# Even mixer of a hybrid encoder: gate weights folded with the block-diagonal ones, v turned by its product, tiles and heads in another order, values centred before attention

## The reference, cut to what matters

```
u_m, z_m, u_r, g_r = _split(x @ w_in, EVEN_SIZES)          # 4 x 1024
# mLSTM half
c = silu(dw_conv(u_m, conv_w, conv_b))
q, k, v = blockdiag(c, wq), blockdiag(c, wk) / 16, blockdiag(u_m, wv)   # blocks of 4
qkv = concatenate([q, k, v], axis=-1)
i_pre = einsum('bld,rdh->rbhl', qkv, w_ig) + b_ig           # r: two directions, h: 4 heads
log_f = log_sigmoid(einsum('bld,rdh->rbhl', qkv, w_fg) + b_fg)
h = chunkwise attention with decays from log_f, i_pre, forward plus backward
y_m = sigmoid(z_m) * head_norm(h, norm_g, ML_HEADS, center=True)        # minus mean, over root of variance
# RG-LRU half
x = dw_conv(u_r, ...); r, i = sigmoid(blockdiag64(x, w_a) + b_a), sigmoid(blockdiag64(x, w_x) + b_x)
a = exp(-8 r softplus(-lam)); h = a h_before + sqrt(1 - a*a) * i * x    # both directions
y_r = (h_f + h_b) * gelu(g_r)
return concatenate([y_m, y_r], axis=-1) @ w_out
```

## Time and profile before

| | |
|---|---|
| time, median of 3 runs | 2589.86 us (2588.8 to 2591.7) |
| the profiled execution | 2589.05 us, its span 2587.3 us |
| mean granted clock of TensorE | 0.982 of 2.4 GHz |
| busy in the span | PE 98%, PEld 81%, DVE 50%, ACT 35%, POOL 40% |
| chain that ended last | PE 85%, DVE 8%, ACT 4%, issue 2% |

### The profile page before, as it was taken

One profiled execution on the slowest core, in us unless ns is written; L12 is line 12 of the kernel. 1 busy time (PEld: TensorE's weight loads), 2 busy tenths in 40 slices (PEclk: granted clock), 3 DMA queues, 4 the chain that ended last, 5 costly groups with the idle time before them and its releaser, 6 DMA issues.

```text
span 2587.3 us, 32687 instructions
## 1 busy us (share of the span) xinstructions
PE 2530.2 (98%) x11838; PEld 2089.5 (81%) x11838; DVE 1283.3 (50%) x1519; ACT 902.0 (35%) x1178; POOL 1047.4 (40%) x484
## 2 busy tenths in 40 slices
PE   8999999999999999999999999999999999999998
PEld 7888887776767888888888888888888788788887
DVE  3333357666566433235333245676777566433335
ACT  3223236675232322213222214444544332422222
POOL 6444453221123544445444445333333333544443
PEclk9999999998999999999999999999999999999999
DMA  4222222111112222322222322222222222222222
GB/s 153 97 97 98 101 70 72 64 62 43 47 49 73 82 94 94 108 95 73 98 97 97 102 98 93 74 74 75 73 74 74 69 78 85 78 97 97 98 101 78
DMA packets 63676, 218.75 MB, mean 85 GB/s; under 512 B 10925, under 2 KB 15021, under 8 KB 63457
## 3 DMA queue, kind: packets, MB, share of 16 engines
q1 hardware_dynamic: 63120, 216.03, 24.5%
q0 software_dynamic: 464, 1.45, 0.2%
HBM read 215.36 MB, written 2.10 MB: 84 GB/s over the span
## 4 chain that ended last, share of the span: by engine, by line
PE 85%; DVE 8%; ACT 4%; issue 2%; POOL 1%; DMA 0%; DVEq 0%; POOLq 0%; ACTq 0%; SPq 0%
PE ps L485 24%; PE ps L486 24%; PE ps L487 24%; PE ps L516 2%; PE ps L935 2%; DVE sb_cv L1737 1%; DVE sb_th L1761 1%; DVE sb_lx L1737 1%; DVE sb_rec L1863 1%; ACT sb_th L1295 1%; PE ps L642 1%; PE ps L641 1%; PE ps L640 1%; PE ps L646 1%; DVE sb_x L1659 1%
## 5 line engine op out<-in xcount | busy, mean ns | idle before, releaser
L394 POOL TENSOR_TENSOR sb_wl<-sb_raw,sb_wh 128x1024 fp32r<-128x1024 f32 (+1 forms) x376 | 974.2, 2591 | 1468.9 <-ACT sb_wh L1108 1468.9
L1108 ACT ACTIVATE sb_wh<-sb_raw 128x1024 fp32r<-128x1024 f32 (+1 forms) x376 | 419.4, 1115 | 1326.7 <-PE ps L487 1264.1
L485 PE MATMUL ps<-sb_xh,sb_wh 128*128 128x512 f32 x2096 | 835.2, 398 | 0.9 <-DVE sb_rq L1986 0.5
L487 PE MATMUL ps<-sb_xl,sb_wh 128*128 128x512 f32 x2096 | 820.4, 391 | 0.0
L486 PE MATMUL ps<-sb_xh,sb_wl 128*128 128x512 f32 x2096 | 820.4, 391 | 0.0
L485 PEld LDWEIGHTS ps<-sb_xh,sb_wh 128*128 128x128 f32 x2096 | 396.6, 189 | 89.5 <-issue 4.6
L487 PEld LDWEIGHTS ps<-sb_xl,sb_wh 128*128 128x128 f32 x2096 | 396.0, 189 | 83.9
L486 PEld LDWEIGHTS ps<-sb_xh,sb_wl 128*128 128x128 f32 x2096 | 396.5, 189 | 82.4 <-issue 3.1
L1571 DVE SCALAR_TENSOR_TENSOR sb_hf<-sb_sg,ps 128x512 f32<-128x512 f32 x88 | 60.5, 688 | 589.8 <-PE ps L487 567.1
L485 PE MATMUL ps<-sb_hh,sb_wh 128*128 128x512 f32 x616 | 239.7, 389 | 0.5 <-POOL sb_wl L394 0.5
L487 PE MATMUL ps<-sb_hl,sb_wh 128*128 128x512 f32 x616 | 239.7, 389 | 0.0
(11 more groups left out here) (337 smaller groups left out, 2980.6 us busy)
## 6 DMA issues: line engine op xcount, KB each, us to landing
sb_raw<-w_in SPq DMA_DIRECT2D x176, 512.0 KB, 3.2
sb_raw<-w_out SPq DMA_DIRECT2D x64, 704.0 KB, 4.0
sb_raw<-w_od SPq DMA_DIRECT2D x80, 512.0 KB, 3.2
sb_raw<-w_ev SPq DMA_DIRECT2D x40, 512.0 KB, 3.2
sb_raw<-w_evo SPq DMA_DIRECT2D x8, 512.0 KB, 3.2
sb_raw<-w_odo SPq DMA_DIRECT2D x8, 512.0 KB, 3.2
sb_x<-x_in SPq DMA_DIRECT2D x8, 256.0 KB, 5.7
out<-sb_x SPq DMA_DIRECT2D x16, 128.0 KB, 1.8
```

The lines of the kernel that those rows point to most:

```text
L394: pool.tensor_tensor(wl[:, sl.par, 0:n], raw[:, sl.par, 0:n], wh[:, sl.par, 0:n].bitcast(F32), ALU.subtract).then_inc(lo_done, 1)
L485: pe.matmul(out, w_h, rh(k), start=start and k == 0, stop=False)
L487: mm = pe.matmul(out, w_h, rl(k), start=False, stop=stop and k == kt - 1)
L1108: act.activation(wh[:, sl.par, 0:kt * P], raw[:, sl.par, 0:kt * P], ACT.Copy).then_inc(hi_done, 1)
```

## The change

The gate products are q·w, k·w and v·w with q = c·wq and so on, so the weights are multiplied once: `wf` holds wq·w + wk·w/16 for c, and wv·w for u_m. It is made by VectorE once, behind the first feed-forward input phase, from a table `wgs` that replaces `wg`. For each tile VectorE copies 32 weights per channel into `gw`, spread so that each gate kind starts at its own partition of 32, and TensorE does two products of 512 columns with them. The gate sums arrive as rows in bank 6, and need no transpose. v is made with `um` as stationary operand and `bd` as moving one, so that it comes out by token, without `vf` and transposes. The tile order is new: slot m of tile t, LRU gate products, slot u of tile t + 1, slot g, inner products; the slots and transfers are dealt in that order. On ScalarE the four tanh stand ahead of Silu, and the stores of q, k, v at the tile's end; on VectorE the scans of a tile follow in the same tile. The mean of a head over its channels is taken out of `vT` (`value_centre`: weights in attention are the same for all channels of a head), so `head_mean` and `head_cen` go. ScalarE stores the head as `k_all`, and its square as `q_all`, straight from PSUM, and VectorE adds the two halves of the square (`square_sum`), so that `head_var` has one product. The slots of z and of the output product lie elsewhere among the heads, keys × queries of the next head stand behind the attention product, and z has two buffers.

```diff
+                def inner(t):
+                    bq, bk, bv = QKV_BANKS
+                    u = um[:, :, 2:2 + L]
+                    pe.wait_ge(bd_done, t + 1)
+                    pe.wait_ge(c_done, t + 1)
+                    pe.wait_ge(u_ev, t + 1)
+                    pe.wait_ge(lt_done, 4 * t + 2)
...
+                    pe.matmul(ps[:, 6, :], gw[:, 0, :], cc[:], start=t == 0, stop=False)
+                    pe.matmul(ps[:, 6, :], gw[:, 1, :], u, start=False, stop=t == KD - 1)
                     for b in range(NB):
+                        o = 2 + (b % SB) * P
+                        mm = pe.matmul(ps[:, bv, b * P:(b + 1) * P], um[:, b // SB, o:o + P], bd[:, 2, :],
+                                       start=True, stop=True)
+                    mm.then_inc(vt_mm, 1)
...
+                    else:
+                        pe.wait_ge(u_ev, t)
+                        of_x(0, sl(ev_m(t)))
+                        lru_gates(t)
+                        if t < KD - 1:
+                            pe.wait_ge(lu_ev, t + 1)
+                            of_x(1, sl(ev_u(t + 1)))
+                        pe.wait_ge(gelu_done, t)
+                        of_x(2, sl(ev_g(t)))
+                    inner(t)
...
+                def value_centre(h):
+                    v = vT[:, :, HT * h * P:HT * (h + 1) * P]
+                    dve.wait_ge(vt_ev, HT * h + HT)
+                    step(dve.tensor_reduce(vmean[:], v, mybir.AxisListType.X, ALU.add))
+                    step(dve.tensor_scalar(vmean[:], vmean[:], 1.0 / (HT * P), None, ALU.mult))
+                    step(dve.tensor_tensor(v, v, vmean[:, :, None].to_broadcast([P, NB, HT * P]), ALU.subtract))
...
+            def head_var(c, bank, src):
+                pe.wait_ge(rsq_done, c + 1)
                 pe.wait_ge(hv_done, c + 1)
+                pe.matmul(ps[:, bank, :], cn("mean_256"), src, start=True, stop=True).then_inc(hvar_mm, 1)
...
+            def square_sum(c, sq):
+                dve.wait_ge(hsq_done, c + 1)
+                dve.tensor_tensor(sq[:, 0, :], sq[:, 0, :], sq[:, 1, :], ALU.add).then_inc(rsq_done, 1)
...
                 for h in range(NH):
                     if h >= 1:
                         pe.wait_ge(hv_done, h)
...
-                    if h >= 1:
-                        head_mean(h - 1, 6, hv, lambda: None)
...
+                    if h == 0:
+                        early_out(1)
+                    elif h == 1:
+                        pe.wait_ge(part_in, 3)
+                        early_out(4)
...
+                    else:
+                        early_out(6)
                     pe.wait_ge(att_done, h + 1)
...
+                    if h < NH - 1:
+                        if h >= 1:
+                            pe.wait_ge(hvar_in, h)
+                        keys_queries(h + 1)
                 pe.wait_ge(z_done, 7)
+                early_out(7, (0, 3))
+                pe.wait_ge(hvar_in, NH - 1)
+                head_var(NH - 1, 7, q_all[:, HT * (NH - 1), :])
+                early_out(7, (3, KD))
```

More of the change, by code:

```diff
@@ L144, in build @@
     lgl = sb("lgl", [P, T], F32, e1)
[L145 removed]
+    e1[0] += 256
     e2 = [e1[0]]
@@ L357, in _, with slot @@
                 elif kind == "even":
+                    def slot(j):
+                        load(slot_of(a["w_ev"], j), KD, Slot(n0, 0, 2, j))
                     for t in range(KD):
-                        for j in (EV_U(t), EV_M(t), EV_G(t)):
-                            load(slot_of(a["w_ev"], j), KD, Slot(n0, 0, 2, j))
+                        if t == 0:
+                            slot(ev_u(0))
+                        slot(ev_m(t))
                         if t == 0:
@@ L368, in _ @@
                                                "c g d -> c g d")).then_inc(bd_in, 16)
+                        for j in sorted([ev_g(t)] + ([ev_u(t + 1)] if t < KD - 1 else [])):
+                            slot(j)
                     stream(a["w_ev"], 3 * KD, 2 * KD, KD, n0 + 3 * KD)
@@ L1270, in even @@
                     act.activation(lum[:, :, 2:2 + L], seqs(ps[:, 1, :]), ACT.Copy).then_inc(lu_ev, 1)
-                    if t >= 1:
-                        decay_root(t - 1)
-                        gelu(t - 1)
-                    split(KD, sl(EV_G(t)))
-                    if t >= 1:
-                        v_turned(t - 1)
-                    used(sl(EV_M(t)))
+                lru_in(0)
+                for t in range(KD):
+                    last = t == KD - 1
+                    if t == 0:
+                        split(KD, sl(2))
+                    used(sl(ev_m(t)))
                     if t == 0:
@@ new lines, in even @@
+                    if t == 0:
+                        split(KD, sl(4))
+                    decay(t)
+                    if not last:
+                        lru_in(t + 1)
+                        split(KD, sl(ev_u(t + 1) + 2))
+                    decay_root(t)
+                    if not last:
+                        gelu(t)
+                        if t >= 1:
+                            split(KD, sl(ev_g(t) + 2))
+                        inner_out(t)
+                    else:
+                        split(KD, sl(ev_g(t) + 2))
@@ L1328, in even @@
                 act.activation(g2[:], g1[:], ACT.Ln, bias=1.0).then_inc(rows_a, 1)
+                for d in range(2):
+                    y = 64 * d
+                    act.activation(gi[:, d, :], ps[y:y + NH, 6, :], ACT.Identity, bias=gb[y:y + NH, 0:1]).then_inc(rows_a, 1)
+                inner_out(KD - 1)
                 split(KD, sl(EV_F[0]))
                 gelu(KD - 1)
+                split(KD, sl(EV_F[1]))
                 act.wait_ge(gT_mm, 1)
@@ L2022, in ret @@
                     dve.wait_ge(rz_done, r + 1)
-                    head_norm(c, 7, rhv, rrec[:], "ret_g", HT * r, rzs, yhB, ylB)
+                    head_norm(c, 7, rhv[:], rrec[:], "ret_g", HT * r, rzs, yhB, ylB)
                     if more:
```

372 lines of the change are left out of this document (170 added, 202 removed).

## The result

The changed kernel takes **2570.16 us** (median of 4 runs, 2568.5 to 2572.8) against 2589.86: a ratio of 0.9926, with a 95% interval of 0.9913 to 0.9938. That is 19.7 us less, where 28.8 were forecast. It lies inside the range (2544 to 2572), near its upper end.

The account below looks back on a forecast made before the run. The prediction took TensorE to bound the kernel nearly everywhere, with slack in the VectorE and ScalarE loop. Tiles −10.0, hand-over −0.8, heads −18.0 and start 0 gave −28.8, about 2561 us against 2589.86; range 2544 to 2572.

Parts of the forecast that it names:

- Tiles, −10.0: Even mixer's eight tiles: seven rounds save 6.4 us and the first tile 3.6, together 10.0 us less.
- the first tile gains more: First tile: three evictions no longer ahead of Exp, 1.4, and only two stalls, 2.2, so 3.6 us less.
- The round of 26.2: One tile's loop through VectorE and ScalarE, ylB to ylB: 20.0 us plus three stalls, 6.2, longer than TensorE's 24.1.
- the tile is TensorE's: Tiles before the change: TensorE's full 27.12 us sets the time; the loop through VectorE and ScalarE has slack.
- Hand-over, −0.8: From the tiles to the heads: work leaves ScalarE, one split is new, both scan stalls stay; 0.8 us less.
- Start, 0 with a bound of +2: Before the tiles: weight folding on VectorE and a larger gate table cost nothing, at most 2 us.
- Heads, −18.0: Four heads: −10.2 removed passes, −7.5 waits, −4.8 low clock, +2.9 new waits, +1.6 clock; 18.0 us less.
- The clock term behind it, +1.6: End of the heads: after the last variance's wait TensorE's clock probably falls once more, costing 1.6 us.
- Rival 1: Tiles: TensorE keeps setting them at 24.1 us because VectorE's stalls fall into idle time; 2546 us, chance 0.17.
- Rival 2: Tiles: round of 27.1 to 27.5 us, from full 2.4 stalls or a dearer gate copy; 2567 to 2570, chance 0.16.
- Rival 3: Heads: only the removed passes come back, −10.2 instead of −18.0; 2569 us, chance 0.12.
- Rival 4: Tiles: TensorE's clock falls over a large part of each tile and the kernel gets slower; 2640 us, chance 0.05.

Follow-up runs that it names:

- e1: Changed kernel with the first tile's slot g load put ahead of the LRU gate weights' transfer in SyncE's queue: 2564.35 us, ratio 0.9906.
- the second profile: The changed kernel run once more, unedited, for another profile: 2569.20 us, ratio 0.9922.
- e2: Changed kernel with GpSimd's subtraction cut from 1024 to 8 columns for the 40 slots up to the end of the heads: 2546.94 us, ratio 0.9838.
- e3: Changed kernel with a second buffer for the scan half of th, and Exp and tanh ahead of Silu from tile 1 on: 2551.01 us, ratio 0.9854.
- e9: Changed kernel without VectorE's centring of the values in tiles 2, 4 and 6: 2571.35 us, ratio 0.9922.
- e8: Changed kernel with GpSimd's subtraction cut to 8 columns for one slot a tile, from tile 1 on: 2558.78 us, ratio 0.9876.
- e11: Kernel before with GpSimd's subtraction cut from 1024 to 8 columns for the 40 slots of the even mixer: 2577.01 us, ratio 0.9952.
- e12: Kernel before with VectorE's copy to yhB written four times instead of once in each tile: 2603.83 us, ratio 1.0051.
- e10: The kernel before run once more, unedited, for a second profile: 2597.24 us in one run.
- e4: Changed kernel with the last head's square sum moved up on VectorE, between the last two operations of head 2's norm: 2566.04 us, ratio 0.9909.

## Why the prediction was right, and where it was not

**The side and the range** were right. The likeliest time was 9 us too low. Between 5 and 6 us of that are one place, the late slot; 1.8 are the longer wait of the last variance, and what remains is within what executions differ by.

**Tiles, −10.0.** The first tile's gain of 3.6 did not come: from lum to its tanh it lost 4.9. The step that failed is "the first tile gains more", which went through ScalarE and VectorE and took the arrival of the slots as given. That slot g's load had moved behind the LRU gate weights, and behind their wait for VectorE's zeros, had no term. It cost 7.6 us in the profile (198.4 against 190.8 in e1; 6.0 by the second profile's 196.8), and 5.8 in the medians. With the slot back in its place the tiles gain 10.1.

**The round of 26.2** measured 26.0 to 26.2. Its parts stood too: three stalls of 2.0 to 2.2, TensorE's side of 24.1 (24.16 in e2 and e3), TensorE's wait of about 2 at slot m (1.7 to 1.8), the covered centring (e9). The Trainium skill, "SBUF — State Buffer", section "SBUF: two separate sides", calls the shared port pair an exclusive lock for the whole instruction, which made 27.2. The rows' smaller number was right for the round, and e8 measures one stall at 2.1. The rows do not speak against a lock: the stretched scan of 532.75 ends 0.5 us behind the end of the subtraction of 532.67 beside it, and loses 2.16 of its 2.36 us. That the subtraction makes the stall is shown by e2 and e8.

One leg of the sum was right by luck. The forecast went from ylB through bd, the copy and the convolution of m to Silu, 3.8 us, and left the four tanh and Silu's table out. In the trace this convolution ends at 515.49, and Silu starts at 515.81 behind the tanh (from 512.07) and the table: 3.74 us on ScalarE set the leg. The two paths happen to be equally long.

**What bounded the kernel before** was wrong. I read TensorE's full row as "the tile is TensorE's" and took the 5.4 and 1.8 us waits of VectorE and ScalarE as slack. They are the ring's own hand-overs: VectorE waits for lum while ScalarE works without a pause, and ScalarE for ylB while VectorE does. e11 (25.5), e12 (28.6) and e10 (27.2 at full clock) show it. The number survived because the forecast set 26.2 against the measured 27.12, ring against ring. But the reason was wrong: the tile did not get shorter by TensorE's passes. From 27.11 to 26.18 ScalarE's part went from 9.12 to 8.76 (three evictions and a split left it, 2.5 us; Silu and its table came in, 2.0), and VectorE's from 17.31 to 16.65 (the convolution of um left it, 2.8; a third stall came in, 2.1). The passes that TensorE lost (a full-clock tile of 25.5 became 24.1) bought nothing there; only without a stall (e2, e8) or with the second buffer (e3) do they count.

**Hand-over, −0.8**: −0.95, with both stalls in the scans, as it said. **Start, 0 with a bound of +2**: +0.8.

**Heads, −18.0**: −16.4 and, with the changed kernel's second profile, −20.6; the second profile of the kernel before (169.8) would add 4.7 to either. So −18.0 is right within what executions differ by, and no run tests it more closely. The attention products no longer wait and run at full clock (14.6 us and 380 ns a pass against the earlier trace rows's 19.2 and 466), the evictions' waits are gone, heads 1 and 2 took 37.7 to 39.3 and 32.2 where 38 and 33 were expected. The last variance waits 3.75 and not 2.0: the term left out a fourth kind of stall, GpSimd's subtraction beside ylA (3.40 instead of 1.23 us). The clock term behind it, +1.6, was right: e4, without the fall, is shorter by 1.7 more than its wait. What the forecast had no term for is the clock at the start of head 3, 3.4 us that come in one execution and not in the other.

**The rivals.** Rival 1 (TensorE keeps the tiles) would have needed one stall fewer, as e8 shows with rounds of 24.0. Rival 2's 27.1 did not come (its figures were also loosely added: the gate copy at its upper bound gives 26.7, not 27.1). Rival 3's time, 2569, is close to the measured one, but for another reason: the heads gave back more than their removed passes. Rival 4's clock did not fall in the tiles (0.98), but for the first one.

## What to carry to other kernels

A full engine is not yet the bound. Follow one period backwards from an instruction to the same instruction a tile earlier: if the sum of work and hand-overs on other engines is the period, the full engine only fills it, and passes taken from it buy nothing. A second execution helps too: here the engine that looked full at a clock of 0.95 waited 1.1 us a tile at 0.99, and the tile was as long.

When slots are dealt anew, write down the load queue of the first tile beside the old one. A load that moves behind a transfer with a wait of its own is late once, and once was 5 to 8 us here.

A subtraction of 2.4 us on GpSimd cost VectorE 2.0 to 2.2 us wherever VectorE was in the ring. Count them in every stretch, the ends of stages too.
